# A streaming encoder step on eight cores: earlier input and pooling, later transposes, and a transpose moved to the DMA

## The reference

```
xn = rmsnorm(x, g_mix_pre);  [u | B | C | h] = xn @ w_in            # 4 x 512 wide
pool: 4 channel groups, window w in (2,4,8,16): mean of last w of u, minus u; @ w_pool[g]; * scale
conv: B * conv3(C * h)                                              # depthwise, causal
x += rmsnorm([norm(pool) | norm(conv)] @ w_out, g_mix_post)
k, v = rmsnorm(mem, g_mem) @ w_k, w_v                               # 256 memory tokens
x += rmsnorm(softmax(q k^T / 16) v @ w_co, g_x_post),  q = rmsnorm(x, g_x_pre) @ w_q
x += rmsnorm(relu(rmsnorm(x, g_ff_pre) @ w_up)^2 @ w_down, g_ff_post)
```

## Time and profile before

| | |
|---|---|
| median of 3 runs | 898.96 us (898.18 to 900.38) |
| the profiled execution | 901.45 us, span of its slowest core 900.1 us |
| spans of the eight cores | 893.8 to 900.1 us |
| granted TensorE clock, mean | 0.989 to 0.998 |
| PE busy | 859.5 us (95%) |
| ACT, DVE busy | 432.4, 448.9 us |

### The profile page before, as it was taken

The page is one execution under the profiler, slowest core; times in us unless marked ns, Lnnn a source line. Parts: engine busy times, 40 slices in busy tenths (PEclk is TensorE's granted clock), DMA queues, the critical chain, the costliest instruction groups (busy, mean ns, idle before and its releaser), DMA issues.

```text
span 900.1 us, 14693 instructions; the slowest of 8 cores (893.8 to 900.1 us)
## 1 busy us (share of the span) xinstructions
PE 859.5 (95%) x5018; PEld 453.0 (50%) x5018; DVE 448.9 (50%) x772; ACT 432.4 (48%) x1043; POOL 53.0 (6%) x66
## 2 busy tenths in 40 slices
PE   7898898999999999999999998999899999999996
PEld 4565444664456666544444443457454444444442
DVE  3788687476872222232142877886684222200133
ACT  4557888466873333332132386886684333200122
POOL 1100100000000000000001000000000000000000
PEclk9989989999999999999999999999999999999998
DMA  9997376719585654636829992171716746426022
GB/s 195 194 155 110 76 118 105 127 28 206 76 151 81 98 80 62 102 88 115 117 100 120 236 228 82 40 96 23 95 21 110 107 69 94 59 36 87 8 94 94
DMA packets 66793, 91.89 MB, mean 102 GB/s; under 512 B 2936, under 2 KB 58360, under 8 KB 66208
## 3 DMA queue, kind: packets, MB, share of 16 engines
q0 software_dynamic: 58080, 60.95, 48.1%
q1 hardware_dynamic: 8640, 30.00, 10.2%
HBM read 137.49 MB, written 12.30 MB: 166 GB/s over the span
## 4 chain that ended last, share of the span: by engine, by line
PE 80%; ACT 9%; issue 4%; DVE 4%; DMA 2%; ACTq 0%; DVEq 0%; SPq 0%; POOLq 0%
PE psum L393 77%; PE psum L397 3%; ACT stg L411 3%; ACT xsb L411 3%; ACT st L411 2%; ACT un L411 2%; DMA ring<-w_in 1%; DMA X<-xp 1%; DVE un L423 1%; DVE xT L414 1%; DMA conv_p<-stg 1%; DVE X L423 0%; DVE un L414 0%; DVE un L418 0%; DVE xsb L418 0%
## 5 line engine op out<-in xcount | busy, mean ns | idle before, releaser
L393 PE MATMUL psum<-xT,ring 128*128 128x352 bf16 (+6 forms) x2336 | 413.0, 333 | 3.6 <-DVE xT L414 2.5
L393 PEld LDWEIGHTS psum<-xT,ring 128*128 128x128 bf16 x2336 | 226.5, 98 | 167.5 <-issue 6.6
L393 PE MATMUL psum<-ring,un 128*128 128x512 bf16 (+1 forms) x1408 | 302.6, 380 | 0.0
L411 ACT ACTIVATE un<-psum 128x352 bf16<-128x352 f32 (+9 forms) x258 | 125.0, 492 | 201.2 <-PE psum L393 198.9
L393 PEld LDWEIGHTS psum<-ring,un 128*128 128x128 bf16 (+1 forms) x1408 | 130.7, 98 | 157.7 <-issue 9.1
L414 DVE TENSOR_TENSOR un<-un 128x352 bf16<-128x352 bf16 (+5 forms) x176 | 84.8, 483 | 156.8 <-ACT un L411 156.8
L414 DVE TENSOR_TENSOR stg<-psum,gp 128x1024 f32<-128x1024 f32 (+3 forms) x51 | 53.1, 1042 | 106.6 <-ACT stg L411 57.6
L411 ACT ACTIVATE stg<-psum 128x1024 bf16<-128x1024 f32 (+3 forms) x51 | 44.5, 873 | 104.8 <-PE psum L393 102.6
L414 DVE TENSOR_TENSOR xT<-psum,gcs 128x1024 bf16<-128x1024 bf16 (+2 forms) x52 | 60.0, 1155 | 35.7 <-PE psum L397 35.2
L393 PE MATMUL psum<-ring,mg 128*128 128x512 bf16 (+1 forms) x320 | 75.8, 388 | 0.0
L423 DVE SCALAR_TENSOR_TENSOR X<-stg,st,X 128x1024 f32<-128x1024 f32 (+3 forms) x51 | 56.3, 1104 | 6.8 <-DVE stg L414 4.7
(11 more groups left out here) (95 smaller groups left out, 517.1 us busy)
## 6 DMA issues: line engine op xcount, KB each, us to landing
ring<-w_up POOLq DMA_DIRECT2D x16, 1024.0 KB, 14.2
ring<-w_down POOLq DMA_DIRECT2D x16, 1024.0 KB, 10.7
X<-xp SPq DMA_DIRECT2D x16, 512.0 KB, 14.0
yp<-X SPq DMA_DIRECT2D x16, 512.0 KB, 2.7
ring<-w_in POOLq DMA_DIRECT2D x7, 1024.0 KB, 11.4
ring<-w_out POOLq DMA_DIRECT2D x4, 1024.0 KB, 31.8
ring<-w_q POOLq DMA_DIRECT2D x4, 1024.0 KB, 22.7
stg<-xp SPq DMA_DIRECT2D x8, 512.0 KB, 4.3
```

The source lines that it names most:

```text
L393: P.add("pe", lambda e: e.matmul(out, lhsT=lhsT, rhs=rhs, start=start, stop=stop), reads=[lhsT, rhs], writes=[out])
L411: P.add("act", lambda e: e.activation(out=out, in_=in_, func=func, scale=scale, **kw), reads=rd, writes=wr)
```

## The change

- The transfer of block 2 waits for block 1 to land, not for the first weight half; the two small tables `ident` and `gcol` are asked for by ScalarE.
- `chain` and `CHAIN` are written anew: steps A, S, T, G of block 2 stand ahead of unit 0, those of block 3 after units 0 and 1. There are five scaled buffers, and they lie where V is written later.
- The pooled sums of group 0 go in three ranges (272, 512 and 288 columns), from units 4, 12 and 16; before in two from 12 and 16. The copies of u on DVE are those of units 4 to 7, before 5, 7, 9 and 11. All maps of group 0 stand earlier.
- Three small DVE additions for `psel` move from the start to phase 3.
- In `out_block`, `pre_b` comes four units after `p2`, before three; `p2` squares into the spent half of `stg`, not into `xsb`; with `in_co` there is no `weave` at a block's end, and `s3` comes two units after `s2`.
- In `hook0` the eight matmul transposes of a block are replaced by one transposing DMA on SP's queue, from `xs` into `xT`; seven units later DVE multiplies the gain in, in place.

```diff
-P_TILES = [[(0, 528), (528, 1072)], [(16, 528), (528, 1040)]]
-P_AT = [(12, 16), (4, 8)]
-MAP_AT = [[[(1, 8), (1, 9), (1, 10), (1, 11)], [(2, 3), (2, 5), (2, 7), (2, 9)], [(2, 11), (3, 0), (3, 2), (3, 4)]],
+P_TILES = [[(0, 272), (272, 784), (784, 1072)], [(16, 528), (528, 1040)]]
+P_AT = [(4, 12, 16), (4, 8)]
+MAP_AT = [[[(1, 3), (1, 5), (1, 7), (1, 9)], [(1, 11), (2, 1), (2, 3), (2, 5)], [(2, 7), (2, 9), (2, 11), (3, 1)]],
-                    ev_u(jj, proj(w, jj, lo, hi), lo, hi, grp == 0 and n in (5, 7, 9, 11))
+                    ev_u(jj, proj(w, jj, lo, hi), lo, hi, grp == 0 and 4 <= n < 8)
@@ pre_a
-        act(xs, Xap, AF.Square, accum=stat(key, 3, r))
+        act(xs if junk is None else junk, Xap, AF.Square, accum=stat(key, 3, r))
@@ out_block
-            xs = pre_a(xb, r, key, par)
-            later(3, lambda: pre_b(xs, r, gi, xT3[:, :, c0 + 16:c0 + 16 + r]))
+            xs = pre_a(xb, r, key, par, None, junk)
+            later(4, lambda: pre_b(xs, r, gi, xT3[:, :, c0 + 16:c0 + 16 + r]))
         later(2, p2)
-        weave()
+        if not in_co[0]:
+            weave()
@@ attn_half
-            later(1, s3)
+            later(1 + in_co[0], s3)
@@ the start
-    dma("sp", idf[:, :], ident[:, :], rd=False)
-    dma("sp", gcs[:, :], gcol[:, :], rd=False)
+    dma("act", idf[:, :], ident[:, :], rd=False)
+    dma("act", gcs[:, :], gcol[:, :], rd=False)
     dma("sp", Xs(1), xrow(0, 1), rd=False)
-    P.add("sp", lambda e: e.dma_start(out=Xs(2), in_=xrow(0, 2)), reads=[first], writes=[Xs(2)], dma=True)
+    P.add("sp", lambda e: e.dma_start(out=Xs(2), in_=xrow(0, 2)), reads=[Xs(1)], writes=[Xs(2)], dma=True)
-    CHAIN = {0: "A3", 2: "A4", 3: "W8 S3 T3 G3 W8 S4 T4 G4 A5 A6 W4", 4: "A7", 5: "S5 T5 S6 G5 A8", 6: "T6 G6", 7: "S7 A9",
-             8: "T7 S8 G7", 9: "T8 G8", 10: "S9", 11: "W3 T9 G9 W2"}
-    chain("W11 A0 A1 S0 T0 G0 W2 A2 S1 T1 G1 W7 S2 T2 G2 W5")
+    CHAIN = {0: "A4", 1: "S4 T4 G4", 2: "A5", 3: "A6", 4: "A7", 6: "S5 W2 T5", 7: "S6 W3 G5 T6 W3 G6 A8",
+             8: "S7 T7 A9", 9: "G7 S8", 10: "T8 G8 S9", 11: "W2 T9 G9 W2"}
+    chain("W11 A0 A1 S0 T0 G0 W2 A2 S1 T1 S2 G1 W3 T2 G2 A3 W6 S3 T3 G3")
@@ hook0
-            later(2, lambda: pre_b(xs, 128, 0, xT3[:, :, xcol(j):xcol(j) + 128]))
+            dst = xT3[:, :, xcol(j):xcol(j) + 128]
+            P.add("sp", lambda e: e.dma_start(out=dst, in_=xs, transpose=True), reads=[xs], writes=[dst], dma=True)
+            later(7, lambda: tt(dst, dst, gcs[:, 0:8].unsqueeze(2).to_broadcast([128, 8, 128]), ALU.mult))
```

More of the change, by code:

```diff
@@ L548, in build_program, with pre_a @@
     xs_rr = [0]
-    def pre_a(Xap, r, key, on_act=False, xs=None):
+    def pre_a(Xap, r, key, on_act=False, xs=None, junk=None):
         if xs is None:
@@ L595, in build_program @@
     S_OFF = P_OFF + 4 * MW * 2
-    SW = [592, 528]
+    SW = [528, 528]
     sA_OFF = S_OFF
@@ L1170, in build_program @@
     memx = [uf(PT_OFF + 8192, 1024), uf(PT_OFF + 12288, 1024)]
-    xs_pro = [ub(P_OFF + 2048 * i, 1024) for i in range(4)]
+    xs_pro = [ub(V_OFF + 2048 * i, 1024) for i in range(5)]
     xs_mem = [ub(KVP_OFF + 2048 * i, 1024) for i in range(2)]
@@ L1194, in build_program @@
     vmemset(ones[:, :], 1.0)
-    vmemset(ub(S_OFF, 512), 1.0)
+    vmemset(ub(65536, 512), 1.0)
     vmemset(bd64[:, :], 0.0)
@@ L1203, in build_program @@
     vcopy(idb[:, :], idf[:, :])
-    tt(psel[:, 0:32], idf[:, 0:32], idf[:, 32:64], ALU.add)
-    tt(psel[:, 0:32], psel[:, 0:32], idf[:, 64:96], ALU.add)
-    tt(psel[:, 0:32], psel[:, 0:32], idf[:, 96:128], ALU.add)
     pre_q = [(halo, 16, 9, 0, xT3[:, :, 0:16])]
@@ L1210, in build_program @@
         pre_q.append((Xs(b), rows(b), skey(b), 0, xT3[:, :, xcol(b):xcol(b) + rows(b)]))
-    pre_xs = [xs_pro[k % 4][0:q[1], :] for k, q in enumerate(pre_q)]
+    pre_xs = [xs_pro[k % 5][0:q[1], :] for k, q in enumerate(pre_q)]
     pre_tb = {}
@@ L1229, in c_g @@
         gain_out(pre_tb.pop(k), r, gi, dst)
-    warm = ub(S_OFF, 512)
+    warm = ub(65536, 512)
     def c_w(n):
@@ L1260, in fill0 @@
                 tt(psg[:, :], pvt[:, 0:4], pvt[:, 16:20], ALU.mult)
+        elif phase == 3 and n == 11:
+            tt(psel[:, 0:32], idf[:, 0:32], idf[:, 32:64], ALU.add)
+            tt(psel[:, 0:32], psel[:, 0:32], idf[:, 64:96], ALU.add)
+            tt(psel[:, 0:32], psel[:, 0:32], idf[:, 96:128], ALU.add)
         elif phase == 2 and n == 0:
```

## The result

| | before | after |
|---|---|---|
| median (lowest to highest) | 898.57 us, 4 runs (897.75 to 900.38) | 909.74 us, 4 runs (908.74 to 910.20) |
| profiled execution, span of the slowest core | 901.45, 900.1 us | 910.20, 908.6 us |
| PE / DVE / ACT busy | 859.5 / 448.9 / 432.4 us | 852.0 / 450.4 / 433.7 us |
| granted TensorE clock, mean of a core | 0.989 to 0.998 | 0.978 to 0.986 |

The account below looks back on a forecast made before the run. TensorE was taken as the bound (four fifths of the chain), ACT close behind in group 0's output blocks. Terms 3.6 + 4.1 + 1.0 + 1.3 + 1.4 + 3.1 + 0 = 14.5 off 901.45, less 2.5: 884.5 us; range 877 to 892.

Parts of the forecast that it names:

- stage_down: Eight blocks of stage_down: matmul transposes leave TensorE, the replacing DMAs are wholly hidden; -3.6 us (bounds -3.6 to +9.2).
- attention, group 1: Group 1 attention output blocks: the 3.22 us wait for DVE scaling and 0.9 us slow clock go; -4.1 us (-5 to 0).
- into stage_up, group 0: Between output blocks and stage_up of group 0: later transposes remove a 0.99 us wait; -1.0 us (0 to -1.4).
- w_out, group 0: Stage with w_out, group 0: transposes one unit later give ACT that unit once; -1.3 us (0 to -3.1).
- w_out, group 1: Stage with w_out, group 1: transposes one unit later, two waits of 2.9 us shortened; -1.4 us (0 to -2.9).
- phases 1 to 3: Phase 3 of group 0: one map instead of three takes 3.1 us off ACT; -3.1 us (0 to -6.2).
- the start: Before unit 12: earlier block 2 and added DVE work taken together as 0 us, bounds -4 to +4.
- -2.5 + 5.2 - 3.4: Start: 2.5 us gained at unit 4, 5.2 us added DVE work, 3.4 us DVE free before unit 12; sum -0.7 us.
- rival C: Start: block 2 takes the weights' turn on the DMA engines, unit 12 some 4 us late; 888.5 us, chance 0.12.
- the reader of `xT` stands at least two units behind: Transposes one unit later: `xT` is still read at least two units after the moved transposes; no size given.
- three half blocks more: Group 1 attention: the later half has three half blocks before its transposes, 5 us and more against a 3.2 us wait.
- Rival B: stage_down: transposing DMAs take turns and are slow, DVE is late and TensorE stops; 909.8 us, chance 0.09.

Follow-up runs that it names:

- 1: Kernel before with only the transposing DMAs of stage_down (`hook0`) changed: 897.42 us, ratio 0.9985.
- 2: Kernel before with the transposing DMAs of stage_down and SP's final waits ordered so the last store is waited for last: 895.45 us, ratio 0.9961.
- experiment 9: Kernel before with only the softmax half moved (no `weave` at a block's end with `in_co`, `s3` later): 895.96 us, ratio 0.9960.
- 10: Kernel before with softmax half and square into `stg`: with transposes four units after `p2` in attention blocks 899.58 us (1.0012); with old transposes 897.12 us (0.9985).
- experiment 8: Changed kernel with the w_out stages' transposes back at three units after `p2`, square into `stg` kept: 905.62 us, ratio 1.0070.
- experiment 7: Kernel before with the change's pooling, maps, copies of u and place of scaled buffers; old requests and step order: 901.98 us, ratio 1.0031.
- experiment 4: Kernel before with only the request order changed, block 2 asked for when block 1 has landed: 903.12 us, ratio 1.0048.

## Why the prediction was wrong, by its steps

| term | forecast | in the change | by itself |
|---|---|---|---|
| stage_down | -3.6 | -3.6 | -3.6 (experiments 1, 2) |
| attention, group 1 | -4.1 | +0.7 | -2.6 (half alone, 9), +0.3 with the transposes (10) |
| into stage_up, group 0 | -1.0 | +0.7 | +0.9 (10) |
| w_out, group 0 | -1.3 | -1.3, then +4.4 | -0.7, then +4.9 (8) |
| w_out, group 1 | -1.4 | -1.2 | -1.0 (8) |
| phases 1 to 3 | -3.1 | -3.3 | -3.6, paid with 6.0 (7) |
| the start | 0 (-4 to +4) | +10.9 | |
| the end | not priced | +1.6 | +1.4 (1) |

The column "in the change" is measured against the one profile of before, which is 0.3 to 0.4 us too long in phases 1 to 3 and in both w_out stages.

**The start is the step that failed most.** "-2.5 + 5.2 - 3.4" took DVE's 3.4 us of idle time as room. It was a sum of idle over 13 us, in pieces between steps that TensorE waits for; DVE executes in order, and the 5.2 us stand ahead of scalings and gains. What counts is what each piece stands in front of: alone it cost 6.0 us (experiment 7), more than its own length, which was 5.8 us there (the four outputs took 0.42 us each and not 0.36). The second piece of that step, 2.5 us from the earlier block 2, had the landing right (3.1 us sooner) and the effect wrong: `chain` had moved its transposes ahead of units 0 and 1, so that these waited. And the requests cost 3.1 (4), which stood under rival C, priced at 4, but with a chance of 0.12 and beside a gain. Then TensorE's longer pauses brought the half clock; the prediction counted that as a gain where a pause goes, and not as a price where new ones come. Where "I take 0" stood, the start lost 10.9 us. Without these the change would have come out level with the kernel before, not 14.5 us under it: the terms below had lost the rest.

**The transposes one unit later** were priced by waits: 0.7 us was gained in w_out of group 0 (forecast 1.3) and 1.0 in group 1 (1.4), by experiment 8. The waits behind the first price lie in the query units and not in the w_out stage, and there 1.9 us of them stayed. The step "the reader of `xT` stands at least two units behind" was counted in TensorE's order. The gain between them is on DVE, 4.6 us behind its transposes (10), and in the query units it stands on DVE behind the scaling of memory tokens (8). That turned -3.7 for these three terms into +2.6 with what they did to the query units, and in group 1 it took back what the softmax half gained.

**The softmax half** had the right sign and was too large: -4.1 where -2.6 is measured. The wait of 3.2 us did go, but "three half blocks more" is not what the edit gives: it moves the scaling and the transposes together and does so for both halves, so that the first half got a wait of 1.82 us. The slow clock was worth 1.2 us in the mean of the cores, from 0 to 2.8, not 0.9; that part depends on the core. In the change all of it was hidden by the transposes' new waits.

**stage_down and phase 3** came out by their sums. The transfers took 8.4 us in the median, 4.6 to 13.2 in the semaphore events, between the two ends that were taken for them. DVE did wait for them, 12.9 us, which the prediction had named as a sign of being wrong; but TensorE waited for nothing there, so it cost nothing. Rival B, which gave 909.8 us, did not happen: the measured time is near it for other reasons. Of the two rules of the Trainium skill weighed there, neither fits exactly: eight pieces by "VectorE: DVE Perf Modes" (The three transpose paths) would by estimate be 10.5 us, and 8.4 us from issue to landing is nearer to that than the plain load's 4.3 us before. "Advanced Engine Details and Errata" (X-Bar Transpose (TRN2)) says that transposing DMAs are as fast as others; the load beside it took 7.8 us in the same profile, nearly the same time, but for twice the bytes (512 KB against 256). Contention can't be told apart from the transpose itself by these runs.

**Open:** whether another order of steps would make the early sums pay; and why the same pause of TensorE is followed by the lower clock on some cores and not on others.

## What to carry to other kernels

Idle time of an engine that works in order is no room for new work: write down, for each added operation, which operation comes next on that engine and who waits for it. When a step is moved, follow its result through every engine to its reader; a distance in one engine's units says nothing if another engine's queue lies between. When a number of units is changed for one step, look at every instance of that step, not only at the one that waits. And leave room in the price of each new long pause of TensorE for the half clock behind it: the pauses of 5.16 and 4.54 us in the change were followed by 1.5 and 1.2 us lost in slow matmuls, that of 1.92 us by 1.7 us on one core and by nothing on seven.

## What the runs showed of the hardware

- A transposing DMA of a 128 x 1024 bf16 block from SBUF to SBUF landed 8.4 us after its issue (median), beside weights on the same engines; the gain in place then took DVE 1.22 us.
- The row blocks and the first weights share the DMA engines though they are on different queues: asking for block 2 and the blocks behind it some 3.4 us earlier let the weights' second half land at 18.9 us, before at 15.7, and TensorE waited 2.83 us for it (experiment 4).
- Waits at the end of the program cost time when they are passed after the last landing: 2.0 us with the last store's near the head (1), 0.29 with it last (2).
- The lower clock level came behind some pauses of TensorE and not behind others of the same length (granted clock of the 3 us behind them, all eight cores). In the change: behind the pauses of 4.5 us near 162 us on all eight (0.50 to 0.54 of full), behind those of 2.8 us in phase 3 on six, behind those of 1.9 us near 651 us on one. In the kernel before: behind the 3.2 us near 646 us on five. In experiment 9: behind the 1.82 us on none.
- At the lower level 16 matmuls took 3.48 us in the change; half of the 32 that took 3.87 before are 1.94.
